# Gate and up of the next expert chunk placed in front of the turn of this chunk's gated rows

## The reference

```python
h = silu(einsum('nd,edf->nef', t, w_gate)) * einsum('nd,edf->nef', t, w_up)
y = einsum('nef,efd->nd', h * comb[:, :, None], w_down)
```

## Time and profile before

| | us |
|---|---|
| Median of 3 runs | 1198.81 (1195.37 to 1199.28) |
| The profiled execution | 1193.71 |
| Its span, first to last instruction | 1191.9 |
| PE busy | 930.2 (78%) |
| DVE, ACT, POOL busy | 366.5, 238.3, 176.6 |

### The profile page before, as it was taken

How to read it: one execution, slowest core, us unless ns; L and a number is a source line. 1 busy time by engine, 2 the same in 40 slices (tenths; PEclk the granted TensorE clock), 3 DMA queues, 4 the chain that set the end, 5 groups by cost and what they waited for, 6 DMA issues and landing times.

```text
span 1191.9 us, 13816 instructions
## 1 busy us (share of the span) xinstructions
PE 930.2 (78%) x5214; PEld 539.9 (45%) x5214; DVE 366.5 (31%) x880; ACT 238.3 (20%) x583; POOL 176.6 (15%) x212
## 2 busy tenths in 40 slices
PE   1699988975899877773699998896588987777642
PEld 1256556542555534431345645553355553443322
DVE  0128644135121111110545836215412111111052
ACT  1210047124011101001140016505111111101023
POOL 4000000001233222223020000000223322221100
PEclk8799989997899999997799998998799999999876
DMA  9972357051799999999488235522299999995521
GB/s 345 394 267 106 117 219 318 1 211 57 275 413 416 413 414 411 413 382 393 175 297 302 105 109 221 219 106 106 106 403 411 415 413 412 412 413 235 220 107 53
DMA packets 83583, 321.86 MB, mean 270 GB/s; under 512 B 13432, under 2 KB 17814, under 8 KB 65344
## 3 DMA queue, kind: packets, MB, share of 16 engines
q1 hardware_dynamic: 68144, 294.14, 62.6%
q0 software_dynamic: 14512, 20.57, 4.9%
q10 hardware_dynamic: 864, 6.29, 1.3%
HBM read 320.93 MB, written 23.59 MB: 289 GB/s over the span
## 4 chain that ended last, share of the span: by engine, by line
PE 53%; SPq 23%; DMA 11%; DVE 7%; ACT 3%; issue 2%; ACTq 0%; POOL 0%; POOLq 0%; DVEq 0%
PE ps L738 12%; PE ps L965 10%; SPq L529 8%; SPq L531 7%; PE ps L918 7%; SPq L536 6%; DMA ring<-in_w_up 5%; PE ps L980 4%; PE ps L741 3%; PE ps L703 3%; DMA arena<-y_pairs 2%; SPq L494 2%; PE ps L900 2%; PE ps L905 2%; DMA ring<-in_w_mod 2%
## 5 line engine op out<-in xcount | busy, mean ns | idle before, releaser
L965 PE MATMUL ps<-ring,tail 128*64 128x256 f32 x1792 | 214.8, 394 | 34.0 <-DMA ring<-in_w_up 32.2
L965 PEld LDWEIGHTS ps<-ring,tail 128*64 128x64 f32 x1792 | 144.0, 142 | 119.6 <-DMA ring<-in_w_up 53.5
L738 PE MATMUL ps<-uT,ring 128*128 128x384 f32 x448 | 151.2, 495 | 4.3 <-DMA ring<-in_w_in 2.7
L1599 DVE TENSOR_TENSOR arena<-arena,ps 128x128 f32<-128x128 f32 x68 | 19.6, 288 | 388.4 <-ACT arena L1226 388.4
L1226 ACT ACTIVATE arena<-ps 128x128 f32<-128x128 f32 x68 | 18.9, 278 | 488.0 <-PE ps L965 488.0
L623 POOL DMA_INDIRECT y_pairs<-tail,row_idx x64 | 64.7, 1010 | 344.5 <-PE ps L973 294.3
L738 PEld LDWEIGHTS ps<-uT,ring 128*128 128x128 f32 x448 | 86.2, 194 | 61.6 <-issue 4.2
L980 PE MATMUL ps<-ring,krow 128*64 128x512 f32 x448 | 108.5, 601 | 3.4 <-issue 2.2
L618 POOL DMA_INDIRECT arena<-u_rows,row_idx x66 | 67.3, 1020 | 38.2 <-issue 37.9
L1356 DVE SCALAR_TENSOR_TENSOR arena<-arena,dw 128x414 f32<-128x414 f32 x118 | 67.6, 644 | 0.0
L703 PE MATMUL ps<-ring,sT 128*32 128x384 f32 x512 | 47.1, 522 | 22.6 <-DMA ring<-in_w_mod 22.6
(11 more groups left out here) (245 smaller groups left out, 977.3 us busy)
## 6 DMA issues: line engine op xcount, KB each, us to landing
ring<-in_w_gate SPq DMA_DIRECT2D x56, 1024.0 KB, 17.4
ring<-in_w_up SPq DMA_DIRECT2D x56, 1024.0 KB, 22.9
ring<-in_w_down SPq DMA_DIRECT2D x56, 1024.0 KB, 23.5
ring<-in_w_mod SPq DMA_DIRECT2D x32, 1536.0 KB, 11.5
ring<-in_w_in SPq DMA_DIRECT2D x8, 1536.0 KB, 18.1
arena<-in_w_gate SPq DMA_DIRECT2D x12, 1024.0 KB, 18.9
arena<-in_w_up SPq DMA_DIRECT2D x12, 1024.0 KB, 24.0
arena<-in_w_down SPq DMA_DIRECT2D x12, 1024.0 KB, 24.1
```

What stands on the lines that cost most here:

```text
L738: last = mm(ps[:, n % 4, 0:T], slot[s][:, k, c:c + P], uT[:, k, :], start=(k == 0), stop=(k == KD - 1))
L965: last = mm(ps[W * half:W * (half + 1), b, 0:2 * P].rearrange("p (j f) -> p j f", j=2), xc[:, b, k, :], gate_up_w[s][:, :, k, half * P:(ha ...
```

## The change

Within the loop over the main chunks on PE, gate_up of chunk i+1, with its three waits, is moved from behind down of chunk i to ahead of the turn of chunk i's gated rows. The lists of the other engines, the buffers, the extra loop and the loads are as they were.

```diff
                 main_gate_up(0)
                 for i in range(NE):
                     b = i % 2
+                    if i + 1 < NE:
+                        main_gate_up(i + 1)
                     wait(h_ready, l, i + 1)
                     wait(hT_ready, l, i - 1)
                     tr(ps[:, 2 + 5 * b, 0:P], hrow[:, b, :], ident).then_inc(h_turned.sem, 1)
...
                     wait(hT_ready, l, i + 1)
                     wait(y_rows, l, i - 1)
                     down(b, i % XRING, down_done)
-                    if i + 1 < NE:
-                        main_gate_up(i + 1)
```

## The result

The changed kernel takes 1201.24 us (median of 8 runs, 1199.52 to 1202.76), the kernel before 1197.06 us (8 runs, 1192.30 to 1199.28). The ratio is 1.0042 with a 95% interval of 1.0022 to 1.0061: slower by 5.0 us by the means of the runs, between 2.6 and 7.3 (4.2 by the medians). The forecast was 6.7 us slower: 1205.5, on a median of 1198.81 for the kernel before from three runs, which over eight runs is 1197.06.

What follows compares the result with a forecast made beforehand. The weight stream, then PE's work after the last landing, was taken as the bound. 2 layers x (1.30 start + 2.04 end) = 6.7 us on the median 1198.81 gave 1205.5; range 1199 to 1212, forecast's chance 0.58 (1202 to 1209).

Steps and rivals of the forecast that it cites:

- rival 1: Start of the stream: the hole is absorbed by the dip at 316, only the end counts; 4.1 us slower, 1202.9; chance 0.20.
- The bound: Expert stages: the weight stream at about 412 GB/s sets their end; a faster PE only eats the lead of filled slots sooner.
- rival 3: Chunks at PE's pace: earlier slot releases speed the stream, each saves 0.69 us; 24 less 4.1, 1179; chance 0.08.
- The start: First reloads of each layer: chunk 5's down load issued 3.0 us later, leaving one 1.30 us hole per layer (bounds 0, 3.0).
- the hole: Load queue after chunk 5's gate load: down load comes 6.39 us later against 5.09 us of queued work, 1.30 us empty.
- a hole in the one queue has nothing to fill it: Argument against the hole at the stream's start being absorbed, so its 1.30 us per layer would count.
- that dip: Weight stream before the change, at 316 us: rate down to 229 GB/s; taking in the hole would make its cost 0.
- The middle: Landing-paced main chunks: PE needs 6.4 us against 8.2 between landings, so the 0.69 us removed becomes longer waiting; cost 0.
- rival 2: Clock falls in the merged wait: gate-and-up 5.36 us, each layer's last and layer 0's extra pay 1.69; 11.8 slower, 1210.6; chance 0.14.
- The end: After each layer's last gate-and-up: two turns and downs remain, G + 5.45 against G + 3.41; +2.04 us (bounds 1.9, 2.3).
- The loads of the next layer's weights: First modulation load issued at 542.3 instead of 534.27, 8 us later, still done ahead of its first user; cost 0.
- that chance: First extra's gate-and-up: 3.67 us in layer 0, 5.36 in layer 1 by clock; 1.69 us a layer either way, taken as 0.

## Why the prediction was right, and what it mis-sized

**The time alone** does not tell the forecast (6.7 us) from rival 1 (4.1): the interval, 2.6 to 7.3, holds both. The parts do.

**The bound: right.** The stream sets the end; its rate did not follow PE's pace, and rival 3's 24 us stayed hidden until the loads were cut.

**The start: seen, and mis-sized.** The delay of the down load is 6.07 - 3.39 = 2.7 us (forecast 3.0), the hole 1.1 to 1.2 us (forecast 1.30). Net, the last gate-and-up starts 0.51 us later in layer 0 and 0.86 in layer 1, counted from the first reload. The step that failed is "a hole in the one queue has nothing to fill it": nothing fills it, but the kernel before has a loss of its own 2 us later, which the hole replaces in part. The prediction had seen that dip and left open what makes it; it is the wait for gate-and-up of chunk 1, which the edit shortens. With 0.5 to 0.9 us a layer the start lies between rival 1 (nothing) and the forecast.

**The middle: free, but the clock was misjudged.** PE still waits for landings, longer, and the releases come in time. I had written that waits of this size would not bring the clock down. They did, in 9 of the changed kernel's main chunks and in none before (chunk 0 aside, which is slow before too). The section of the Trainium skill that the prediction cites there (TensorE: Matmul & The Clock Gate, "Loop structure matters more than you think") speaks of a long wait, a word that the prediction left out; here the clock fell behind one of 1.92 us in layer 1. So the mechanism of rival 2 was there, but not its price: such a chunk costs nothing while it is followed by a shorter wait, and the last gate-and-up took 3.67 us in both layers. In layer 1 the clock fell at chunk 30, so that PE's own work ended just when the last landing came; but the weight load (PEld) of the last gate-and-up was still released by that landing, so without the slow chunk it would have started no earlier. Its 0.86 us is the stream's.

```profile
1086.58 5.36 PE L965 MATMUL ps<-ring,tail 128*64 128x256 f32 x32 [1.92 <-DMA ring<-in_w_up]
...
1094.36 3.22 PEld L965 LDWEIGHTS ps<-ring,tail 128*64 128x64 f32 x32 [0.68 <-DMA ring<-in_w_up]
...
1094.37 3.67 PE L965 MATMUL ps<-ring,tail 128*64 128x256 f32 x32
...
1105.89 3.67 PE L965 MATMUL ps<-ring,tail 128*64 128x256 f32 x32 [0.87 <-DVE tail L1594]
```

**The end: right.** +1.86 us for a forecast of 2.04, just under its lower bound of 1.9. The loads of the next layer's weights cost nothing, as forecast: they are issued from 541.89 on (forecast 542.3), and their first user starts at 598.54 without a wait. The first extra's gate-and-up is slow now in layer 0 (547.01) and fast in layer 1 (1105.89), the reverse of before, so that chance cancelled in these profiles.

**The sum.** 2 x 1.86 + 0.51 + 0.86 = 5.1 us in place of 6.7; of the 1.6 us between, 1.2 lie at the start and 0.4 at the end.

## What to carry to other kernels

In this kernel, where a weight stream sets the pace of the stage, the order on the compute engine lost or won only at the stream's two ends. Where a stream sets the pace, ask what the first reloads wait for, and what is left to do when the last weights have landed. Look at the order of the loads together with the order of the work: this edit lost 0.4% with the old load list and won 0.25% with a list written for it, though most of that gain is the place of the last loads, and the new list with the old order was not run. A schedule that is one step behind pays that step at the end, and going back costs it as well unless there is slack to work it off in.

## What the runs showed of the hardware that was not expected

The granted clock fell behind single waits of 1.9 to 3.1 us for a landing, though the matmul work of each chunk around them was the same as before, when two waits of 1.1 and 0.7 us left it at 2.4 GHz throughout. In the changed kernel's timeline and stretches of 2 us (the clock is the third figure from the end, 0.50 is 1.2 GHz):

```profile
454.37 5.36 PE L965 MATMUL ps<-ring,tail 128*64 128x256 f32 x32 [1.96 <-DMA ring<-in_w_up]
462.56 3.67 PE L965 MATMUL ps<-ring,tail 128*64 128x256 f32 x32 [0.20 <-DMA ring<-in_w_up]
```

```profile
452.00:454.00 2.00, 0.41 (x2) 0.00 (x0) 0.00 (x0) 0.60 (x1) 0.00 (x0) 1.00 1.01 404
456.00:458.00 2.00, 2.00 (x12) 1.15 (x10) 0.00 (x0) 0.00 (x0) 0.55 (x1) 0.50 1.03 424
```

The slow chunk takes 5.36 us, the next wait shrinks to 0.20 us, and the clock is back. It does not fall each time: most waits of 1.7 to 2.0 us passed without it, and so did one of 3.39 us (ahead of 412.66). With the x turn ahead it fell once in the main chunks, behind a wait of 2.89 us; the waits there of up to 1.87 us, most of them about 1.3, all left it at 2.4 GHz:

```profile
415.39 5.36 PE L965 MATMUL ps<-ring,tail 128*64 128x256 f32 x32 [2.89 <-DMA ring<-in_w_up]
```
